# Three more buffers for the scan groups' convolution input, VectorE's chunk 0 additions moved ahead of a convolution, and two PSUM evacuations moved ahead of two silus

## Chip, cores and metric

The kernel runs on one core of a Trainium2 chip. The metric is the device time of one execution in microseconds (us), the median of several runs. The kernel before takes 1314.83 us (3 runs, 1314.35 to 1315.46).

## What is computed

A backbone of two trunk layers over 256 context and 256 latent tokens of width 1024, all in one launch. Layer 0 mixes tokens by a bidirectional Mamba-2 scan, layer 1 by differential attention, and each is followed by a SwiGLU FFN. The change lies in the scan of layer 0. Cut to what matters:

```python
def project(h):                                   # h: rmsnorm and modulation of x
    zxbcdt = h @ w_in                             # 1024 -> z 2048, x 2048, B and C 4 x 128 each, dt
    xbc = silu(dwconv_centred(xbc, conv_w, conv_b))   # 5 taps along the tokens, per channel
def ssd_scan(x, dt, a, b, c, h0):                 # chunks of 128 tokens, 4 groups of 8 heads
    cb = einsum('bclgn,bcsgn->bgcls', cc, bc)
    wmat = cb[:, :, None] * _segsum_exp(a_cum)
    y_diag = einsum('bghcls,bcsghp->bclghp', wmat, xd)          # within a chunk
    states = einsum('bclgn,bclghp->cbghpn', bc, xd * decay_states[..., None])
    y_off = einsum('bclgn,cbghpn->bclghp', cc, h_prev) * decay_out[..., None]   # from the state
# y = y_diag + y_off, forward and backward, + x * d_skip, * silu(z), rmsnorm, @ w_out
```

## The kernel before

The weights arrive as units of 128x2048 f32 (1 MB). ScalarE makes the high f16 half `wh` of each (L408), VectorE the low half `wl` (L854), and TensorE multiplies a unit in eight k-steps of six matmuls (`gemm`, L1501 to L1503), which write two PSUM banks.

The scan runs by groups g = 0 to 3. Groups 0 to 2 are a loop of three iterations, in each of which TensorE computes group g's scan and, interleaved with it, the projection of group g+1: four units, k = 0 to 3. Units 0 to 2 give the six pre-activation tiles of group g+1 (tile 0 is B, 1 is C, 2 to 5 are x), two a unit, and unit 3 gives z. Group 3 (`last_group`, `more=False`) has three z units. The scan's small matmuls hang on the k-steps as hooks, so that TensorE meets them in a fixed order: `exponents(c, q)` (L1684, L1688) for chunk c and quarter q, `within(c, hq)` (L1703), the product within chunk c for half hq of the heads, `from_states(c)` (L1714) and `y_turn(c)` (L1725), a transposition. `within(1, 0)` is in the hook after unit 1's last k-step, `y_turn(1)` after k-step 1 of unit 2, `within(2, 0)` after its k-step 5, `y_turn(2)` and two `exponents` after its k-step 7, `within(2, 1)` after k-step 0 of unit 3, `from_states(3)` and `exponents(3, 2)` after its k-step 1, `within(3, 0)` after k-step 2.

Every engine works through an instruction order written by hand, and the engines meet in semaphores alone.

- ScalarE: `exps` (four 128x128 exponentials, L481), `evac_pre` (copies a tile from PSUM to the buffer `pre`, L452), `silu_xbc` (L472), `z_out` (silu of z from PSUM, L488), and `cvt`, the halves of a unit (L408). The exponentials and the silus have different activation tables, loaded in turn (ACT_TABLE_LOAD).
- VectorE: `conv_tile` (one TENSOR_SCALAR, L1011, and four SCALAR_TENSOR_TENSOR, L1015, from a pre-activation tile into `acc`), `half_chunk(g, c, q)` (L1076, L1078: the factors that `within(c, q)` multiplies), `off` (L1087, L1090), `from_state(g, c)` and `from_chunk(g, c)` (L1060, L1068: add the two parts of y of chunk c into G) and `cvt` (L854).
- GpSimd: the summands of the states, and the gate of a finished group (L1471), which waits for the group's last `from_chunk`. In the last group VectorE's preparation, and with it the first `exponents`, waits for that gate.

Chunk c's product within the chunk goes to the one bank YB, and so `within(c+1, 0)` waits until `from_chunk(g, c)` has read it:

```python
if hq == 0:
    pe.wait_ge(yb_ok, g * NCH + (c + 1))
```

In the loop `pre` has two buffers, tile t using number t mod 2, and the evacuation of tile t waits for the convolution of tile t-2 (`conv_ok`). For group 0's projection, ahead of the loop, `first_pre` gives tiles 2 to 4 three buffers of their own, `px`, in a part of `x` that is not in use until the scan is over. Unit k+1 begins when both tiles of unit k are evacuated (`pre_ok`). A convolution waits for its tile and for the silu of the tile before the last, whose `acc` buffer it takes:

```python
ve.wait_ge(pre_ok, n + 1)
if not (isinstance(g, int) and tile < 2):
    ve.wait_ge(xbc_ok, n - 1)
```

Of the kernel before, what the change touches and what calls it, by code (L numbers as in the profile page):

```python
# [118 lines left out]
def build(nc, cols, keep, stage, xT, wada, wadaT, crow, wdt, wxg, wz, wout, wgu, wdn, wv, wqk, wo, out):  # L119
    ctx = ExitStack()  # L120
    with ctx:
# [209 lines left out]
        HN = {0: 0, 2: 1, 3: 2, 4: 3}  # L331


        def first_pre(tile):

            return px[:, tile - 2] if 2 <= tile < 5 else pre[:, tile % 2]

# [60 lines left out]
        def _(act):  # L398
# [49 lines left out]
            def evac_pre(u, g, tile, b):  # L448

                act.wait_ge(unit_done, u.half + (UD + 2))  # L450
                act.wait_ge(conv_ok, g * 6 + (tile + 1))
                act.activation(pre[:, tile % 2, :, 2:258], GB[b][:, :].rearrange("p (s t) -> p s t", s=2), ACT.Copy,  # L452
                               scale=1.0 / (WS * AS)).then_inc(pre_ok, 1)

            def evac_first(u, tile, b):

                act.wait_ge(unit_done, u.half + (UD + 2))
                if tile == 5:
                    act.wait_ge(conv_ok, 2 + 2)
                act.activation(first_pre(tile)[:, :, 2:258], GB[b][:, :].rearrange("p (s t) -> p s t", s=2), ACT.Copy,  # L460
                               scale=1.0 / (WS * AS)).then_inc(pre_ok, 1)

            def z_first(k, banks):
# [4 lines left out]
            def silu_xbc(g, tile):  # L468
                act.wait_ge(conv_ok, g * 6 + (tile + 3))
                if tile == 0 and not isinstance(g, int):  # L470
                    act.wait_ge(xD_ok, g * QT)
                act.activation(xbc[:, tile, :], acc[tile % 2], ACT.Silu).then_inc(xbc_ok, 1)  # L472

            def exps(g, c, q):

                n = g * 16 + (4 * c + q)
                d, hq = q % 2, q // 2
                act.wait_ge(d_mm, n + 1)
                act.wait_ge(yd, g * 8 + (2 * c + hq + 1))
                for h in range(4):  # L480
                    i = act.activation(E[:, hq, d, h, :], DB[q % 2][:, h * P:(h + 1) * P], ACT.Exp, scale=1.0 / DS,  # L481
                                       bias=PRg[:, NEGA, 2 * c + d, 4 * hq + h:4 * hq + h + 1])
                i.then_inc(e_ok, 1)
# [34 lines left out]
            def group(g, u):  # L518

                prepare(g, u)  # L520
                exps(g, 0, 2)
                ada_load(g * 2 + (ADA_FIRST + 1), g * 2 + 1)
                first_states(g)
                exps(g, 0, 3)
                evac_pre(u, g + 1, 0, 0)
                evac_pre(u, g + 1, 1, 1)
                ada_parts(g)
                cvt(u.plus(2))
                for q in range(3):
                    exps(g, 1, q)  # L530
                evac_pre(u.plus(1), g + 1, 2, 0)
                evac_pre(u.plus(1), g + 1, 3, 1)
                exps(g, 1, 3)
                silu_xbc(g + 1, 0)
                silu_xbc(g + 1, 1)
                cvt(u.plus(3))
                for q in range(4):
                    exps(g, 2, q)
                silu_xbc(g + 1, 2)
                silu_xbc(g + 1, 3)  # L540
                evac_pre(u.plus(2), g + 1, 4, 0)
                evac_pre(u.plus(2), g + 1, 5, 1)
                cvt(u.plus(4))
                for q in range(4):
                    exps(g, 3, q)
                silu_xbc(g + 1, 4)
                act.wait_ge(g_ok, g * 2 + 1)
                z_out(u.plus(3))
                silu_xbc(g + 1, 5)
# [103 lines left out]

            u = Unit(U_SSD0)
            act.wait_ge(pads_ok, 3)
            evac_first(u, 0, 0)
            evac_first(u, 1, 1)
            cvt(u.plus(2))

            act.wait_ge(dtv, 1)  # L660
# [2 lines left out]
            act.activation(de, de, ACT.Exp, scale=-1.0).then_inc(dta, 1)  # L663
            act.activation(da, cc("alog"), ACT.Exp).then_inc(dta, 1)
            silu_xbc(0, 0)
            evac_first(u.plus(1), 2, 2)
            evac_first(u.plus(1), 3, 3)
            cvt(u.plus(3))
            ldt = PR[:, LDT].rearrange("p c h -> p (c h)")
            act.wait_ge(adt_ok, 1)  # L670
            act.activation(ldt, ldt, ACT.Ln).then_inc(ln_ok, 1)
            silu_xbc(0, 1)
            evac_first(u.plus(2), 4, 0)
            evac_first(u.plus(2), 5, 1)
            cvt(u.plus(4))
            act.wait_ge(at_mm, 1)
            for d in range(2):
# [164 lines left out]
        def _(ve):  # L842
# [155 lines left out]
                lo0(k)  # L998
            cvt(Unit(U_SSD0 + 1))

            def conv_tile(g, tile, src=None):

                src = pre[:, tile % 2] if src is None else src
                n = g * 6 + tile
                base = g * 36 + tile * 6
                cw = cc("conv")
                ac = acc[tile % 2].rearrange("p (s t) -> p s t", s=2)
# [3 lines that stand above are left out]
                ve.tensor_scalar(ac, src[:, :, 0:TC], cw[:, bass.ds(base, 1)], cw[:, bass.ds(base + 5, 1)],  # L1011
                                 ALU.mult, ALU.add).then_inc(conv, 1)
                for j in range(1, 5):
                    ve.wait_ge(conv, n * 4 + j)
                    ve.scalar_tensor_tensor(ac, src[:, :, j:j + TC], cw[:, bass.ds(base + j, 1)], ac, ALU.mult,  # L1015
                                            ALU.add).then_inc(conv if j < 4 else conv_ok, 1)
# [4 lines left out]
            db = cc("dtb")  # L1021
            ve.scalar_tensor_tensor(dx.rearrange("p (c h) -> p c h", c=NCH), OB[0][:, 0:256].rearrange("p (c h) -> p c h", c=NCH),
                                    1.0 / (WS * AS), db[:, None, :].to_broadcast([P, NCH, 64]), ALU.mult, ALU.add).then_inc(dtv, 1)
            conv_tile(0, 0, first_pre(0))
            cvt(Unit(U_SSD0 + 2))
            ve.wait_ge(dta, 2)
            step(ve.tensor_scalar(dr, de, 2.0, None, ALU.add))
# [35 lines left out]
            def from_chunk(g, c):  # L1063

                ve.wait_ge(yd, g * 8 + (2 * c + 4))
                ve.wait_ge(a_free, g * A_PER + (A_YT[c] + 2))
                gs = G[:, bass.ds(g * QT, QT), c * P:(c + 1) * P]
                ve.tensor_tensor(gs, gs, YB[:, :].rearrange("p (q l) -> p q l", q=QT), ALU.add).then_inc(yb_ok, 1)  # L1068
# [57 lines left out]
            def group(g, u, more):  # L1126
# [20 lines left out]
                off(g, 0)  # L1147
                cvt(u.plus(2))
                half_chunk(g, 1, 0)
                if more:  # L1150
                    conv_tile(g + 1, 1)
                else:
                    add_z(1)
                from_state(g, 0)
                from_chunk(g, 0)
                off(g, 1)
                half_chunk(g, 1, 1)
                if more:
# [29 lines left out]
                from_chunk(g, 3)  # L1188

            u = Unit(U_SSD0)  # L1190
            conv_tile(0, 1, first_pre(1))
            cvt(u.plus(3))
            conv_tile(0, 2, first_pre(2))
            cvt(u.plus(4))
            ve.wait_ge(A_mm, 1)
            ve.wait_ge(aexp, 2)
# [5 lines left out]
            for d in range(2):  # L1202
                ve.wait_ge(at_hi, d + 1)
                ve.tensor_tensor(atr[0:AROWS, d, :], (YB, AB)[d][0:AROWS, :], AT[0:AROWS, d, :], ALU.subtract).then_inc(at_rest, 1)
            conv_tile(0, 3, first_pre(3))
            for d in range(2):
                ve.wait_ge(at_mid, 2 * d + 2)
                ve.tensor_tensor(AT[64:AROWS, d, :], atr[64:AROWS, d, :], atm[64:AROWS, d, :], ALU.subtract).then_inc(at_ok, 1)
            conv_tile(0, 4, first_pre(4))
            cvt(u.plus(5))  # L1210
            conv_tile(0, 5, first_pre(5))
            ve.wait_ge(aexp, 3)
            ve.wait_ge(at_ok, 2)
            with ve.Fori(0, NG - 1) as g:
# [803 lines left out]
```

## Time and profile before

| | |
|---|---|
| median of 3 runs | 1314.83 us (1314.35 to 1315.46) |
| the profiled execution: its own time, its span | 1321.15 us, 1319.5 us |
| mean granted TensorE clock | 0.949 |
| TensorE matmul busy | 1183.2 us (90%) |
| VectorE busy | 896.2 us (68%) |
| ScalarE busy | 589.4 us (45%) |
| GpSimd busy | 90.0 us (7%) |

Busy times are of one profiled execution. The three iterations of the scan loop stand at about 96.4 to 180.6, 180.6 to 264.7 and 264.7 to 348.9 us of the span, and group 3 from there to about 432 us. In a timeline, the time in brackets is how long the engine was idle ahead of the instruction, and behind it what ended the idle time.

### The profile page before, as it was taken

How to read it: one execution, taken by the hardware profiler on the slowest of the kernel's cores; microseconds unless marked ns; L12 is line 12 of the kernel's file. 1: busy time of each engine (PE TensorE's matmuls, PEld its weight loads, DVE VectorE, ACT ScalarE, POOL GpSimd, SP SyncE). 2: the span in 40 equal slices, each digit the busy share in tenths (PEclk: the TensorE clock that was granted, in tenths of full speed). 3: DMA queues.
4: the chain of work that ended last, by engine and by line, in shares of the span. 5: the costliest groups of instructions: out<-in, count | busy, mean ns of one | idle time of the engine just before them, and what ended most of it. 6: DMA issues, size and time to landing. Idle time of an engine off the chain costs nothing.

```text
span 1319.5 us, 20163 instructions
## 1 busy us (share of the span) xinstructions
PE 1183.2 (90%) x7132; PEld 677.1 (51%) x7132; DVE 896.2 (68%) x1395; ACT 589.4 (45%) x1028; POOL 90.0 (7%) x102
## 2 busy tenths in 40 slices
PE   4999898898986699699999999997999968799997
PEld 2545354454443344244444444446745537688886
DVE  5695766858766886888787887537256756666554
ACT  5564654645646432333343332223335534566642
POOL 0004023050230000000000000000000000000000
PEclk9999899999998799899999999997999968899998
DMA  9332121121222244164554645321231102355552
GB/s 388 132 101 91 64 108 52 64 95 64 93 100 95 97 164 182 37 254 186 195 203 182 241 142 220 125 97 64 83 109 64 64 0 96 128 195 208 196 197 96
DMA packets 24526, 173.93 MB, mean 132 GB/s; under 512 B 2720, under 2 KB 2720, under 8 KB 5536
## 3 DMA queue, kind: packets, MB, share of 16 engines
q1 hardware_dynamic: 18432, 128.24, 26.5%
q0 software_dynamic: 4608, 33.56, 7.1%
q10 hardware_dynamic: 1440, 11.53, 2.4%
q8 instruction: 28, 0.46, 0.1%
q14 instruction: 18, 0.15, 0.0%
HBM read 172.27 MB, written 1.05 MB: 131 GB/s over the span
## 4 chain that ended last, share of the span: by engine, by line
PE 79%; DVE 13%; ACT 4%; issue 3%; DMA 0%; DVEq 0%; ACTq 0%; POOL 0%; SPq 0%; POOLq 0%
PE bank L1501 21%; PE bank L1503 20%; PE bank L1502 20%; PE bank L1674 2%; DVE wl L854 1%; PE bank L1856 1%; PE bank L1703 1%; PE bank L1870 1%; DVE arena L931 1%; DVE arena L1015 1%; DVE arena L926 1%; PE bank L1714 1%; PE bank L1843 1%; DVE ssq L913 1%; PE bank L1684 1%
## 5 line engine op out<-in xcount | busy, mean ns | idle before, releaser
L1501 PE MATMUL bank<-hh,wh 128*128 128x512 f16 (+1 forms) x1136 | 392.3, 345 | 25.6 <-DVE hl L922 8.1
L854 DVE SCALAR_TENSOR_TENSOR wl<-raw,wh 128x1024 f16<-128x1024 f32 x224 | 267.5, 1209 | 209.6 <-ACT wh L408 207.4
L1502 PE MATMUL bank<-hl,wh 128*128 128x512 f16 (+1 forms) x1136 | 391.1, 344 | 0.0
L1503 PE MATMUL bank<-hh,wl 128*128 128x512 f16 (+1 forms) x1136 | 390.8, 344 | 0.0
L408 ACT ACTIVATE wh<-raw 128x1024 f16<-128x1024 f32 x224 | 229.3, 1043 | 297.7 <-PE bank L1503 233.6
L1501 PE MATMUL bank<-arena,wh 128*128 128x512 f16 (+1 forms) x544 | 182.4, 335 | 7.2 <-DVE arena L1275 2.8
L1502 PE MATMUL bank<-arena,wh 128*128 128x512 f16 (+1 forms) x544 | 182.4, 335 | 0.0
L1503 PE MATMUL bank<-arena,wl 128*128 128x512 f16 (+1 forms) x544 | 182.2, 335 | 0.0
L1501 PEld LDWEIGHTS bank<-hh,wh 128*128 128x128 f16 x1136 | 112.4, 99 | 130.8 <-issue 48.4
L1503 PEld LDWEIGHTS bank<-hh,wl 128*128 128x128 f16 x1136 | 112.3, 99 | 93.1 <-issue 5.2
L1502 PEld LDWEIGHTS bank<-hl,wh 128*128 128x128 f16 x1136 | 112.3, 99 | 81.2 <-issue 8.9
L884 DVE SCALAR_TENSOR_TENSOR arena<-arena,araw 128x1024 bf16<-128x1024 f32 x128 | 149.0, 1219 | 0.2
L481 ACT ACTIVATE arena<-bank,arena 128x128 f32<-128x128 f32 x256 | 71.5, 377 | 99.9 <-PE bank L1688 99.7
L1501 PEld LDWEIGHTS bank<-arena,wh 128*128 128x128 f16 x544 | 53.7, 99 | 49.0 <-issue 7.4
L1015 DVE SCALAR_TENSOR_TENSOR arena<-arena,col 128x512 f32<-128x512 f32 x84 | 67.3, 802 | 11.8 <-DVE arena L1011 3.0
L1503 PEld LDWEIGHTS bank<-arena,wl 128*128 128x128 f16 x544 | 53.7, 99 | 39.6 <-issue 1.1
L1502 PEld LDWEIGHTS bank<-arena,wh 128*128 128x128 f16 x544 | 53.7, 99 | 39.1 <-issue 0.8
L723 ACT ACT_TABLE_LOAD x22 | 28.2, 1283 | 46.2 <-PE bank L1503 45.8
L1076 DVE TENSOR_TENSOR arena<-arena 128x512 f32<-128x512 f32 x32 | 23.5, 735 | 32.7 <-ACT arena L481 32.2
L1514 PE MATMUL bank<-kp,ssq 128*128 128x1 f32 x40 | 8.2, 324 | 41.1 <-DVE ssq L913 41.1
L1484 POOL DMA_DIRECT2D arena<-wadaT x30 | 15.8, 528 | 380.4 <-DVE arena L884 380.4
L1843 PE MATMUL bank<-wh,hh 128*128 128x256 f16 x128 | 36.1, 282 | 5.6 <-DVE hl L922 4.6
(229 smaller groups left out, 1338.3 us busy)
## 6 DMA issues: line engine op xcount, KB each, us to landing
raw<-wgu SPq DMA_DIRECT2D x44, 1024.0 KB, 4.8
arena<-wadaT POOLq DMA_DIRECT2D x32, 1024.0 KB, 5.1
raw<-wdn SPq DMA_DIRECT2D x16, 896.0 KB, 4.6
raw<-wxg SPq DMA_DIRECT2D x12, 1024.0 KB, 5.0
arena<-wada SPq DMA_DIRECT2D x8, 1024.0 KB, 19.6
raw<-wz SPq DMA_DIRECT2D x8, 1024.0 KB, 4.8
araw<-wada ACTq DMA_DIRECT2D x8, 1024.0 KB, 4.8
raw<-wout SPq DMA_DIRECT2D x8, 1024.0 KB, 4.9
```

Of the source, the lines that this page charges most:

```text
L408: act.activation(wh[:, u.slot, a:b], raw[:, u.slot, a:b], ACT.Copy, scale=WS).then_inc(hi_done, 1)
L481: i = act.activation(E[:, hq, d, h, :], DB[q % 2][:, h * P:(h + 1) * P], ACT.Exp, scale=1.0 / DS, bias=PRg[:, NEGA, 2 * c + d, 4 * hq + h: ...
L723: act.activation(sg[:, m, t0:T], GB[m][:, t0:T], ACT.Silu, scale=1.0 / (WS * AS)).then_inc(sg_ok, 1)
L854: ve.scalar_tensor_tensor(wl[:, u.slot, a:b], raw[:, u.slot, a:b], WS, wh[:, u.slot, a:b], ALU.mult, ALU.subtract).then_inc(lo_done, 1)
L884: i = ve.scalar_tensor_tensor(adump[:, 2 * m + c, :], abuf[:, b, m, :], 1.0, araw[:, c * D:(c + 1) * D], ALU.mult, ALU.mult, accum_out=asu ...
L1015: ve.scalar_tensor_tensor(ac, src[:, :, j:j + TC], cw[:, bass.ds(base + j, 1)], ac, ALU.mult, ALU.add).then_inc(conv if j < 4 else conv_ok, 1)
L1076: ve.tensor_tensor(E[:, q, 0], E[:, q, 0], E[:, q, 1], ALU.add).then_inc(tsum, 1)
L1501: pe.matmul(o, wh[:, u.slot, wsl], ahi[:, k, t0:t1], start=st, stop=False)
L1502: pe.matmul(o, wh[:, u.slot, wsl], alo[:, k, t0:t1], start=False, stop=False)
L1503: i = pe.matmul(o, wl[:, u.slot, wsl], ahi[:, k, t0:t1], start=False, stop=en)
L1674: pe.matmul(OB[b][:, :], Bt[:, c * P:(c + 1) * P], xdd[:, k % 2, :], start=True, stop=True).then_inc(o_mm[b], 1)
L1843: pe.matmul(o, hh[:, k, tk], wh[:, u.slot, w_], start=(k == 0), stop=False)
```

## The change

`pre_tile` takes the place of `first_pre` in all groups: tiles 2, 3 and 4 go to the three `px` buffers, and 0, 1 and 5 to `pre`. `evac_pre` takes the place of `evac_first`. The evacuation of tile 0 now waits for the last convolution of the group before, the one of tile 5 for the convolution of tile 1, and those of tiles 1 to 4 for none. On ScalarE, in the loop, the evacuations of tiles 4 and 5 stand in front of the silus of tiles 2 and 3. On VectorE, `from_state(g, 0)` and `from_chunk(g, 0)` stand in front of the convolution of tile 1 (in the last group, in front of `add_z(1)`, two additions to a sum of squares, L913).

```diff
-        def first_pre(tile):
+        def pre_tile(tile):
             return px[:, tile - 2] if 2 <= tile < 5 else pre[:, tile % 2]
...
             def evac_pre(u, g, tile, b):
                 act.wait_ge(unit_done, u.half + (UD + 2))
-                act.wait_ge(conv_ok, g * 6 + (tile + 1))
-                act.activation(pre[:, tile % 2, :, 2:258], GB[b][:, :].rearrange("p (s t) -> p s t", s=2), ACT.Copy,
-                               scale=1.0 / (WS * AS)).then_inc(pre_ok, 1)
-            def evac_first(u, tile, b):
-                act.wait_ge(unit_done, u.half + (UD + 2))
+                if tile == 0:
+                    act.wait_ge(conv_ok, g * 6 + 2)
                 if tile == 5:
-                    act.wait_ge(conv_ok, 2 + 2)
-                act.activation(first_pre(tile)[:, :, 2:258], GB[b][:, :].rearrange("p (s t) -> p s t", s=2), ACT.Copy,
+                    act.wait_ge(conv_ok, g * 6 + (2 + 2))
+                act.activation(pre_tile(tile)[:, :, 2:258], GB[b][:, :].rearrange("p (s t) -> p s t", s=2), ACT.Copy,
                                scale=1.0 / (WS * AS)).then_inc(pre_ok, 1)
...
                 for q in range(4):
                     exps(g, 2, q)
+                evac_pre(u.plus(2), g + 1, 4, 0)
+                evac_pre(u.plus(2), g + 1, 5, 1)
                 silu_xbc(g + 1, 2)
                 silu_xbc(g + 1, 3)
-                evac_pre(u.plus(2), g + 1, 4, 0)
-                evac_pre(u.plus(2), g + 1, 5, 1)
                 cvt(u.plus(4))
...
-            def conv_tile(g, tile, src=None):
-                src = pre[:, tile % 2] if src is None else src
+            def conv_tile(g, tile):
+                src = pre_tile(tile)
...
                 half_chunk(g, 1, 0)
+                from_state(g, 0)
+                from_chunk(g, 0)
                 if more:
                     conv_tile(g + 1, 1)
                 else:
                     add_z(1)
-                from_state(g, 0)
-                from_chunk(g, 0)
                 off(g, 1)
```

## Rows read from the trace of the kernel before

**Rows 1.** The page: the chain that ended last, share of the span.

```profile
PE 79%; DVE 13%; ACT 4%; issue 3%; DMA 0%; DVEq 0%; ACTq 0%; POOL 0%; SPq 0%; POOLq 0%
```

**Rows 2.** Waits in the three loop iterations: who for whom, total us, times, longest.

```profile
PE bank L1703 <- DVE arena L1068: 13.3, 3, 4.4
...
PE bank L1501 <- ACT arena L452: 6.9, 3, 2.7
```

**Rows 3.** Timeline of TensorE, second iteration: start, length, instruction, idle ahead.

```profile
223.69 1.12 PE L1703 MATMUL bank<-arena 128*64 128x128 f32 x8 [4.44 <-DVE arena L1068]
...
228.72 0.60 PE L1725 MATMUL bank<-kp,arena 128*128 128x128 f32 x4
...
238.17 0.66 PE L1703 MATMUL bank<-arena 128*64 128x128 f32 x8
...
245.97 0.39 PE L1501 MATMUL bank<-hh,wh 128*128 128x512 f16 x1 [2.69 <-ACT arena L452]
...
247.49 1.12 PE L1703 MATMUL bank<-arena 128*64 128x128 f32 x8
...
254.39 0.66 PE L1703 MATMUL bank<-arena 128*64 128x128 f32 x8
...
264.46 0.39 PE L1501 MATMUL bank<-hh,wh 128*128 128x512 f16 x1 [1.25 <-ACT arena L488]
```

**Rows 4.** Timeline of VectorE, second iteration.

```profile
218.09 0.54 DVE L1011 TENSOR_SCALAR arena<-arena,col 128x512 f32<-128x512 f32 x1
...
222.16 0.68 DVE L1060 TENSOR_TENSOR arena<-bank,arena 128x512 f32 x1
...
223.55 0.68 DVE L1087 TENSOR_TENSOR arena<-bank,arena 128x512 f32<-128x512 f32 x1
226.99 0.69 DVE L1076 TENSOR_TENSOR arena<-arena 128x512 f32<-128x512 f32 x1 [2.76 <-ACT arena L481]
...
244.12 0.68 DVE L1076 TENSOR_TENSOR arena<-arena 128x512 f32<-128x512 f32 x1
```

**Rows 5.** VectorE by groups from convolution 1 on: second, then third iteration.

```profile
L1076 DVE TENSOR_TENSOR arena<-arena 128x512 f32<-128x512 f32 x5 | 3.4, 688 | 4.1 <-ACT arena L481 4.1
...
L1076 DVE TENSOR_TENSOR arena<-arena 128x512 f32<-128x512 f32 x5 | 3.4, 686 | 2.3 <-ACT arena L481 2.3
...
L1011 DVE TENSOR_SCALAR arena<-arena,col 128x512 f32<-128x512 f32 x5 | 2.7, 541 | 1.2 <-ACT arena L472 0.8 <-ACT arena L452 0.4
```

**Rows 6.** Timeline of ScalarE around the evacuations of tiles 4 and 5.

```profile
241.87 1.28 ACT L472 ACT_TABLE_LOAD   x1
243.16 0.63 ACT L472 ACTIVATE arena<-arena 128x512 f32<-128x512 f32 x1
...
244.77 1.07 ACT L452 ACTIVATE arena<-bank 128x512 f32<-128x512 f32 x2
245.73 2.00 ACT L408 ACTIVATE wh<-raw 128x1024 f16<-128x1024 f32 x2
```

**Rows 7.** Windows behind three waits: us, busy time by engine, granted clock.

```profile
223.69:228.70 5.01, 5.01 (x25) 2.65 (x26) 1.92 (x3) 2.86 (x6) 0.00 (x0) 0.70 0.00 0
...
245.97:250.80 4.83, 4.83 (x20) 2.13 (x21) 4.15 (x7) 4.80 (x10) 0.00 (x0) 0.65 0.00 0
...
329.78:333.10 3.32, 3.32 (x21) 1.64 (x22) 2.74 (x5) 3.29 (x4) 0.00 (x0) 1.00 0.00 0
```

**Rows 8.** Timeline of TensorE: first iteration, and the first matmul behind it.

```profile
138.53 1.12 PE L1703 MATMUL bank<-arena 128*64 128x128 f32 x8 [4.44 <-DVE arena L1068]
...
180.37 0.39 PE L1501 MATMUL bank<-hh,wh 128*128 128x512 f16 x1 [1.25 <-ACT arena L488]
```

**Rows 9.** Timelines of the last group: VectorE, then TensorE.

```profile
382.63 1.48 DVE L913 TENSOR_TENSOR ssq<-ssq,sq 128x512 f32<-128x512 f32 x2
...
385.65 0.66 PE L1703 MATMUL bank<-arena 128*64 128x128 f32 x8 [3.06 <-DVE arena L1068]
```

**Rows 10.** Window of the last group behind that wait.

```profile
385.65:388.80 3.15, 3.15 (x19) 1.62 (x20) 1.12 (x2) 1.14 (x4) 0.00 (x0) 0.73 0.04 16
```

More of the change, by code:

```diff
@@ L655, in _ @@
             act.wait_ge(pads_ok, 3)
-            evac_first(u, 0, 0)
-            evac_first(u, 1, 1)
+            evac_pre(u, 0, 0, 0)
+            evac_pre(u, 0, 1, 1)
             cvt(u.plus(2))
@@ L665, in _ @@
             silu_xbc(0, 0)
-            evac_first(u.plus(1), 2, 2)
-            evac_first(u.plus(1), 3, 3)
+            evac_pre(u.plus(1), 0, 2, 2)
+            evac_pre(u.plus(1), 0, 3, 3)
             cvt(u.plus(3))
@@ L672, in _ @@
             silu_xbc(0, 1)
-            evac_first(u.plus(2), 4, 0)
-            evac_first(u.plus(2), 5, 1)
+            evac_pre(u.plus(2), 0, 4, 0)
+            evac_pre(u.plus(2), 0, 5, 1)
             cvt(u.plus(4))
@@ L1023, in _ @@
                                     1.0 / (WS * AS), db[:, None, :].to_broadcast([P, NCH, 64]), ALU.mult, ALU.add).then_inc(dtv, 1)
-            conv_tile(0, 0, first_pre(0))
+            conv_tile(0, 0)
             cvt(Unit(U_SSD0 + 2))
@@ L1190, in _ @@
             u = Unit(U_SSD0)
-            conv_tile(0, 1, first_pre(1))
+            conv_tile(0, 1)
             cvt(u.plus(3))
-            conv_tile(0, 2, first_pre(2))
+            conv_tile(0, 2)
             cvt(u.plus(4))
@@ L1204, in _ @@
                 ve.tensor_tensor(atr[0:AROWS, d, :], (YB, AB)[d][0:AROWS, :], AT[0:AROWS, d, :], ALU.subtract).then_inc(at_rest, 1)
-            conv_tile(0, 3, first_pre(3))
+            conv_tile(0, 3)
             for d in range(2):
@@ L1208, in _ @@
                 ve.tensor_tensor(AT[64:AROWS, d, :], atr[64:AROWS, d, :], atm[64:AROWS, d, :], ALU.subtract).then_inc(at_ok, 1)
-            conv_tile(0, 4, first_pre(4))
+            conv_tile(0, 4)
             cvt(u.plus(5))
-            conv_tile(0, 5, first_pre(5))
+            conv_tile(0, 5)
             ve.wait_ge(aexp, 3)
```

## The prediction

> **What bounds the kernel now.** I read the page's chain first: TensorE carries 79% of it and VectorE 13% [rows 1], so a time counts only where TensorE waits or its clock is down. The list of waits over the three loop iterations comes next. Two waits in it belong to this change: TensorE's L1703 for VectorE's L1068, once an iteration and 4.4 us each, and L1501 for ScalarE's evacuation L452, once an iteration, 6.9 us in all [rows 2]. The timelines place them. The first is `within(1, 0)`: VectorE has finished `half_chunk(1, 0)` when it starts convolution 1 at 218.09, and TensorE stands idle from 219.25 to 223.69 because the two additions that free YB come behind that convolution [rows 3, 4]. The second is the start of unit 3, behind silus 2 and 3 and their table load on ScalarE [rows 3, 6]. Last, the windows show the clock: behind a long wait it is granted at 0.70 and 0.65, that is at the 1.2 GHz level for part of the time, but behind the third iteration's evacuation wait, of 2.1 us, it stayed at 1.00 [rows 2, 7]. So some waits cost more than their idle time: 5.01 x 0.30 = 1.5 us and 4.83 x 0.35 = 1.7 us in the second iteration [rows 7].
>
> **Part 1: the additions in front of convolution 1.** Nothing is added; the pair takes the convolution's place. It is as long as from 222.16 to 223.55, 1.4 us, and the convolution 4.07 us (218.09 to 222.16) [rows 4]. Their input, `y_turn(0)`, is ready before 218.09 in this trace, so `from_chunk(1, 0)` ends 4.07 us earlier and TensorE restarts at 223.69 - 4.07 = 219.62: 0.4 us of wait is left of 4.44. TensorE gains 4.07 us, and the 1.5 us of low clock if a wait of 0.4 us leaves the clock up. No row has so short a wait; the nearest are 1.25 us, behind which a matmul takes 0.39 us as at full clock (at half clock it would be longer), and the third iteration's 2.1 us, both without loss [rows 2, 3, 7]. So I take none.
>
> Late next is `off(1)`. It stands behind both pieces and so stays at 223.55 to 224.23 [rows 4]. `y_turn(1)` reads what it writes: TensorE would come there at about 223.3 (219.62, and 5.03 us less 1.4 of low clock [rows 3]) and waits about 1.0 us until 224.3. It is then 228.72 - 224.3 = 4.4 us ahead of before.
>
> **Part 2: VectorE from there on.** Before, VectorE waited on the way: 2.76 us for the exponentials of `half_chunk(1, 1)` [rows 4], and 0.8 us for silu 0 (the third iteration's row; the second lost as much), in all 4.1 + 0.8 = 4.9 us to the iteration's end [rows 5]. These inputs now come earlier than VectorE does: ScalarE has the exponentials by about 222, VectorE reaches them at 224.2. So VectorE works without a break from 218.09 on, and that sets TensorE's pace. At `within(2, 0)` VectorE is ahead by 2.76 + 0.8 = 3.5 us and some tenths, so TensorE starts it at 238.17 - 3.6 = 234.6, after waiting some 0.8 us. At `half_chunk(2, 1)` (244.12 to 245.5 [rows 4]) it is still 3.6 us ahead, so done at 241.9.
>
> **Part 3: evacuations 4 and 5 in front of silus 2 and 3, and the buffers.** Each side issues the same instructions. ScalarE finished the exponentials of chunk 2 at 241.87, 3.7 us behind TensorE's 238.17 [rows 3, 6], so now at 234.55 + 3.7 = 238.2; TensorE ends unit 2 at about the same time (one `within`, two k-steps and one `exponents` behind 234.55), and the two evacuations (1.07 us [rows 6]) no longer wait for the table load (1.28 us) and two silus (1.6 us from 243.16 to 244.77, the wait for convolution 3 in it). Unit 3 starts at about 239.5, where TensorE arrives just then: the wait of 2.69 us is gone, and the lead is 245.97 - 239.5 = 6.5 us. It can't be kept. `within(2, 1)`, one k-step (1.3 us) later, needs `half_chunk(2, 1)` at 241.9: a wait of 1.0 us, lead 247.49 - 241.95 = 5.5. Queued behind the evacuations on ScalarE are silu 2, for which convolution 4 waits, and `cvt`. Silu 2 is done at 239.4 + 1.28 + 0.63 = 241.3 [rows 6], and VectorE comes to convolution 4 at 241.8: covered, by 0.5 us only. If that cover goes, each us later delays VectorE by as much. `cvt` starts after silu 3, at 241.9 instead of 245.73 [rows 6], and the exponentials of chunk 3 move up by 3.9 us; `exponents(3, 2)` may wait 0.7 us for them, but `within(3, 0)` would wait as long for VectorE anyhow. There VectorE, 3.8 us ahead, ends `half_chunk(3, 0)` at 248.75: lead 254.39 - 248.75 = 5.6. From here TensorE finds all inputs ready. The next group begins at 264.46 - 5.6 = 258.8; VectorE's last addition starts 4.9 to 5.2 us earlier. The next iteration's first half is led by TensorE, so it moves whole.
>
> What the three added buffers do is let evacuation 3 follow 2 at once, where it waited for convolution 1. Without them the pair's new place would have made unit 2 wait. Their cost is nothing: the same instructions at another address; a loss would only show as longer L452, L1011 or L1015. The dropped waits were, but for tile 3's, over when ScalarE came to them, and the new ones (tiles 0 and 5) are on convolutions long done. SP's queue isn't touched; its loads follow VectorE's `cvt`, which comes earlier. ScalarE's `ada_load` moves with its silu 5, GpSimd's gate with the last addition.
>
> **Part 4: the other iterations and the last group.** I take restart to next group as in the second, 258.82 - 219.62 = 39.2 us. First: 138.53 - 4.07 + 39.2 = 173.7 against 180.37 [rows 8], 6.7 us, as it had more low clock before. Third: VectorE idled only 2.3 + 1.2 = 3.5 us there [rows 5], which is what can be won, 3.5 to 3.7; the last group's preparation hangs on VectorE's last addition, over GpSimd's gate, so that end decides. In the last group `add_z(1)` goes behind the pair: 1.4 us (two L913 of 1.48 us in all [rows 9]) off a wait of 3.06. Behind it the clock was 0.73, 3.15 x 0.27 = 0.85 us [rows 10]; with 1.7 us of wait I expect it to stay up.
>
> **Sum:** 6.7 + 5.6 + 3.7 + 1.4 + 0.85 = 18.3 us, of the profiled execution's 1321.15 us (span 1319.5): 1.4%. The median of the runs is 6.3 us lower; I take the gain over unscaled, 1314.8 - 18 = 1296.8, so 1297.
>
> A price worth setting down: without the silu swap, unit 3 would start near 242.3, but `within(3, 0)` still waits for VectorE until 248.75. By idle time the swap is worth some 0.3 us an iteration, not 2.3; what it mainly saves is the low clock behind that wait.
>
> **Rivals.**
>
> The clock. The change turns two long waits into five or six short ones, 0.4 to 1.05 us, some 3 us apart. For a loss: 2.69 us cost 1.7 us. Against it: 1.25 and one 2.1 us wait cost nothing [rows 3, 7]. If the clock falls once an iteration for 5 us, as now, 1.5 to 1.7 us are lost, part of it where TensorE would wait anyway: 18.3 - 3 x 1.6 - 0.85 = 12.6, 1302 us. The Trainium skill speaks for this rival, in TensorE: Matmul & The Clock Gate, "A second HAM failure mode: psum-queue depth-cycling": an engine that idles briefly but often between groups of matmuls had its clock swing between the levels. By that rule the time is this rival's or the next one's; no row here shows it so far.
>
> Slower: the same, taken to its end. If the short waits hold the array at 1.2 GHz from the first (223.3) to the last (248.75), some 21 us of matmul time becomes 42, less the 4 us of waiting it fills: 17 us an iteration, 51 in all, 1297 + 51 = 1348. It turns the sign once low clock eats 6 us an iteration, 12 us of TensorE's work at 1.2 GHz, twice what a 4.44 us wait brings now.
>
> More. VectorE is not the next bound and all waits vanish: 13.3 + 6.9 idle [rows 2], about 9 of clock, 2.3 of the last group: 31 us, 1284. Against: the 41 us of VectorE work behind 218.09 (46.0 less 4.9 [rows 5]) need to be done.
>
> Less. A late input that I count as ready, silu 2 above all (0.5 us of cover), costs 1 to 2 us an iteration: 13 to 15 us of gain, 1300 to 1302.
>
> **How the numbers follow.** Forecast (gain 15 to 21.5 us) 0.66; clock, once an iteration, 0.13; less 0.12; more 0.04; no effect beyond the measurement, which tells 0.2% (2.6 us) from nothing, 0.02; slower 0.03. The range takes in the first three: low 1293 (18.3, the third iteration too at 5.6, and 1.5 for a clock loss that goes elsewhere), high 1303. Faster 0.95, same 0.02, slower 0.03.
>
> **What would show it.** L1703 behind `half_chunk(1, 0)` waits 0.4 us and not 4.4; a new wait of 1 us for L1087 ahead of L1725; none or tenths for L452; waits near 1 us of L1703 for L1076 or L1068; VectorE without a wait for 40 us; granted clock near 1.00 in the loop's second halves; iterations of about 77.5, 78.5 and 80.5 us instead of 84. It is wrong if the clock drops in these stretches, if convolution 4 waits for silu 2, or if the stages behind the scan give the time back.

## The result, and the profile after

The changed kernel takes 1301.03 us (median of 4 runs, 1300.25 to 1302.79) where the kernel before takes 1315.14 us (4 runs, 1314.35 to 1316.03): 14.1 us less. The ratio is 0.9882, with a 95% interval of 0.9867 to 0.9897. The forecast was 1297, with a range of 1293 to 1303: the time lies in the range, and the gain is about four fifths of the 18 us that were forecast. The two profiled executions stand further apart, 19.6 us (spans of 1319.5 and 1299.9 us); that difference is the subject of a part below.

The edits shift the line numbers by three to five (other kernels' a little differently): L1703 is now L1698, L1068 L1063, L1076 and L1078 are L1071 and L1073, L1087 is L1082, L1725 L1720, L1501 L1496, L452 L455, L472 L467, L481 L476. TensorE's timeline in the second iteration of the kernel after, which answers to [rows 3]:

```profile
211.83 0.66 PE L1698 MATMUL bank<-arena 128*64 128x128 f32 x8 [0.41 <-DVE arena L1063]
...
216.58 0.65 PE L1720 MATMUL bank<-kp,arena 128*128 128x128 f32 x4 [0.95 <-DVE arena L1082]
...
226.88 0.66 PE L1698 MATMUL bank<-arena 128*64 128x128 f32 x8 [0.73 <-DVE arena L1063]
...
231.93 0.39 PE L1496 MATMUL bank<-hh,wh 128*128 128x512 f16 x1
...
234.32 0.66 PE L1698 MATMUL bank<-arena 128*64 128x128 f32 x8 [0.93 <-DVE arena L1073]
...
238.67 0.39 PE L1679 MATMUL bank<-negm,idb 128*128 128x512 bf16 x1 [0.57 <-ACT arena L476]
...
241.23 0.66 PE L1698 MATMUL bank<-arena 128*64 128x128 f32 x8 [0.65 <-DVE arena L1073]
...
251.29 0.39 PE L1496 MATMUL bank<-hh,wh 128*128 128x512 f16 x1 [1.25 <-ACT arena L483]
```

Read it against the plan of the prediction: 0.4 us in place of 4.44 at `within(1, 0)`; 0.95 of a new wait for `off(1)` (forecast 1.0); 0.73 at `within(2, 0)` (0.8); unit 3 at 231.93 without a wait for the evacuations; 0.93 at `within(2, 1)` (1.0); 0.57 for the exponentials (0.7); and 0.65 at `within(3, 0)`, where the plan had TensorE wait for VectorE too. From the restart at 211.83 to the next group at 251.29 are 39.46 us (39.2). The iteration, from the first iteration's end at 172.54 on, is 78.75 us.

VectorE in the same stretch, by groups, which answers to [rows 5]; the last column is its idle time and what ended it:

```profile
L1010 DVE SCALAR_TENSOR_TENSOR arena<-x,col,arena 128x512 f32<-128x512 f32 x12 | 9.0, 751 | 1.8 <-DVE arena L1006 0.2 <-DVE arena L1010 0.2
...
L1071 DVE TENSOR_TENSOR arena<-arena 128x512 f32<-128x512 f32 x5 | 3.4, 687 | 0.1
...
L1006 DVE TENSOR_SCALAR arena<-x,col 128x512 f32<-128x512 f32 x3 | 1.6, 541 | 0.0
```

L1071 (L1076 before), which stood behind ScalarE for 4.1 us, has 0.1 us of idle time now, and L1006, which waited 0.8 us for silu 0 before, none. What idle time is left lies between the taps of a convolution. The convolutions that read `x` in place of `pre` take 541 and 751 ns an instruction, as before.

The windows of the three stretches from restart to next group (us, busy time by engine, granted clock), which answer to [rows 7]:

```profile
211.80:251.30 39.50, 34.39 (x210) 17.06 (x210) 36.01 (x51) 26.02 (x56) 0.00 (x0) 1.00 0.19 69
133.00:172.50 39.50, 34.38 (x209) 17.05 (x209) 36.01 (x52) 26.05 (x56) 0.00 (x0) 1.00 0.20 70
290.60:330.00 39.40, 34.37 (x209) 17.05 (x210) 35.91 (x51) 25.97 (x56) 0.00 (x0) 1.00 0.18 68
```

Six waits of 0.4 to 0.95 us in each left the clock at 1.00. In the last group the wait of 3.06 us [rows 9] is one of 1.66, and the clock behind it, 0.73 before [rows 10], is full:

```profile
367.60:371.00 3.40, 3.36 (x26) 2.13 (x27) 2.62 (x5) 1.14 (x4) 0.00 (x0) 1.00 0.39 164
```

### The profile page after: what moved, and what is told of

Same layout as the page of the kernel before. It is cut to its first block, busy times and chain, and to the rows that moved or that the text cites. A ratio compares the mean times of both kernels' runs of the same rounds, so it can differ in the third digit from the quotient of the medians.

```text
span 1299.9 us, 20157 instructions
## 1 busy us (share of the span) xinstructions
PE 1172.0 (90%) x7132; PEld 671.7 (52%) x7132; DVE 895.7 (69%) x1395; ACT 589.2 (45%) x1028; POOL 90.0 (7%) x102
## 4 chain that ended last, share of the span: by engine, by line
PE 77%; DVE 13%; ACT 4%; issue 4%; DVEq 0%; DMA 0%; ACTq 0%; POOL 0%; SPq 0%; POOLq 0%
PE bank L1496 21%; PE bank L1498 20%; PE bank L1497 20%; PE bank L1669 2%; DVE arena L1010 1%; PE bank L1851 1%; DVE wl L849 1%; PE bank L1865 1%; DVE arena L926 1%; DVE arena L921 1%; PE bank L1698 1%; PE bank L1838 1%; ACT wh L408 1%; PE bank L1840 1%; PE bank L1839 1%
## 5 line engine op out<-in xcount | busy, mean ns | idle before, releaser
L1496 PE MATMUL bank<-hh,wh 128*128 128x512 f16 (+1 forms) x1136 | 388.8, 342 | 18.6 <-DVE hl L917 8.1
L1496 PE MATMUL bank<-arena,wh 128*128 128x512 f16 (+1 forms) x544 | 182.4, 335 | 7.2 <-DVE arena L1270 2.8
L1496 PEld LDWEIGHTS bank<-hh,wh 128*128 128x128 f16 x1136 | 111.7, 98 | 122.0 <-issue 38.3
L476 ACT ACTIVATE arena<-bank,arena 128x128 f32<-128x128 f32 x256 | 71.1, 380 | 90.0 <-PE bank L1683 89.8
L1496 PEld LDWEIGHTS bank<-arena,wh 128*128 128x128 f16 x544 | 53.7, 99 | 49.1 <-issue 7.4
L1509 PE MATMUL bank<-kp,ssq 128*128 128x1 f32 x40 | 8.2, 324 | 40.8 <-DVE ssq L908 40.8
L1010 DVE SCALAR_TENSOR_TENSOR arena<-arena,col 128x512 f32<-128x512 f32 x48 | 40.3, 840 | 6.5 <-DVE arena L1006 2.0
L908 DVE TENSOR_TENSOR ssq<-ssq,sq 128x512 f32<-128x512 f32 (+1 forms) x55 | 34.6, 628 | 8.7 <-ACT sq L440 3.2
```

Source lines behind the costliest of these rows:

```text
L908: ve.tensor_tensor(ssq[:, t0:T], ssq[:, t0:T], sq[:, b, t0:T], ALU.add).then_inc(ssd, 1)
L1496: pe.matmul(o, wh[:, u.slot, wsl], ahi[:, k, t0:t1], start=st, stop=False)
```

## The experiments

The kernel before was run anew beside these experiments, on the same chip. Its medians there were 1316.2, 1316.9 and 1317.5 us, so the ratios compare better than the times do. Each diff is against the changed kernel, but for the needless work, which went into both kernels.

### The kernel before once more

No edit.

> The kernel before, unchanged, for a second trace of it. Against the two profiled executions the change took 19.6 us off the span, against the medians 14 to 15.5 us. Theory: the profiled execution of before (1321.15 us) had more low clock than most; a new trace near 1315 us has the same waits of TensorE to 0.1 us (4.4 and 2.1 to 2.7 us an iteration), and shorter stretches behind them, so loop iterations of 82 to 84 us where they were 84.0, 84.1 and 82.2. Rival: the 5 us lie elsewhere (loads, the stages behind the scan), and the iterations are again 84 us. Time equal to before within 0.2%.

1316.35 us, ratio 1.0008 (0.9995 to 1.0022). The trace itself missed the expectation: it was again of a long execution (1321.05 us, span 1319.4), with iterations of 84.1 us. But this code was executed 31 times in all, and the granted clock of each is known. The six lines below are the four longest and the two shortest; the shortest four all have a clock of 0.956, and no execution lies between 1318.6 and 1320.9 us.

```
time us   span us   granted clock
1321.18   1319.5    0.949
1321.09   1319.4    0.949
1321.05   1319.4    0.951
1320.94   1319.3    0.949
1314.39   1312.7    0.956
1314.20   1312.5    0.956
```

One program, 1314.2 to 1321.2 us, and the long ones are those of low clock. The trace under the prediction was one of the long ones. No short execution of this code was traced; the next run has a trace of a short execution of the kernel that differs from it in the buffers alone.

### Five buffers alone

```diff
-                evac_pre(u.plus(2), g + 1, 4, 0)
-                evac_pre(u.plus(2), g + 1, 5, 1)
                 silu_xbc(g + 1, 2)
                 silu_xbc(g + 1, 3)
+                evac_pre(u.plus(2), g + 1, 4, 0)
+                evac_pre(u.plus(2), g + 1, 5, 1)
...
-                from_state(g, 0)
-                from_chunk(g, 0)
                 if more:
                     conv_tile(g + 1, 1)
...
+                from_state(g, 0)
+                from_chunk(g, 0)
```

> Five buffers alone, all orders as before. Theory: evacuation 3 goes 2.3 us earlier while TensorE waits for the additions anyway: no change, within 0.2% of before, and each iteration as long as before's. Rival: an earlier evacuation 3 or a convolution source in x changes something of its own: over 0.2% either way, or L1011/L1015 longer than 0.54 and 0.75 us.

1317.53 us, ratio 1.0003 (0.9991 to 1.0014): nothing, as expected. Its trace has a span of 1314.2 us and the waits of before, but for the evacuation wait of the second iteration, 2.12 us and not 2.69. TensorE in its third iteration:

```profile
302.72 0.66 PE L1698 MATMUL bank<-arena 128*64 128x128 f32 x8 [4.45 <-DVE arena L1063]
...
324.69 0.39 PE L1496 MATMUL bank<-hh,wh 128*128 128x512 f16 x1 [2.13 <-ACT arena L455]
341.56 0.38 PE L1496 MATMUL bank<-hh,wh 128*128 128x512 f16 x1 [1.22 <-issue]
```

And the windows from restart to next group (the column behind the busy times is the granted clock), of this kernel first, then of the kernel before from the run above:

```profile
137.20:177.10 39.90, 36.53 (x209) 18.21 (x209) 32.71 (x46) 25.26 (x54) 0.00 (x0) 0.93 0.16 54
220.50:259.40 38.90, 35.52 (x210) 17.76 (x210) 32.72 (x46) 25.26 (x54) 0.00 (x0) 0.96 0.16 54
302.70:341.50 38.80, 35.49 (x209) 17.76 (x209) 32.64 (x46) 25.26 (x54) 0.00 (x0) 0.96 0.16 54
```

```profile
138.10:180.00 41.90, 38.50 (x209) 18.86 (x209) 33.30 (x48) 25.35 (x55) 0.00 (x0) 0.88 0.16 51
223.30:264.10 40.80, 36.84 (x209) 18.41 (x209) 33.21 (x48) 25.46 (x55) 0.00 (x0) 0.92 0.15 51
307.50:346.30 38.80, 35.49 (x209) 17.74 (x209) 32.61 (x46) 25.26 (x54) 0.00 (x0) 0.96 0.15 54
```

The same work, with waits that differ by 0.6 us at most, takes 38.8 to 38.9 us where the clock is 0.96 and up to 41.9 where it is 0.88. The first two iterations together are 3.9 us longer in the long execution.

### The silu swap undone

```diff
-                evac_pre(u.plus(2), g + 1, 4, 0)
-                evac_pre(u.plus(2), g + 1, 5, 1)
                 silu_xbc(g + 1, 2)
                 silu_xbc(g + 1, 3)
+                evac_pre(u.plus(2), g + 1, 4, 0)
+                evac_pre(u.plus(2), g + 1, 5, 1)
```

> The changed kernel with the silus of tiles 2 and 3 back in front of evacuations 4 and 5. Theory (VectorE's unbroken work sets the pace): TensorE waits 2.8 us for the evacuations again, but the waits of 0.93 and 0.57 us behind it vanish, and within(3, 0) is late by 0.3 us only: 1 us over the loop, plus 1.6 us wherever the clock falls behind the 2.8 us wait, 3 of them at most. 1302 to 1307 us. Rival (a wait removed is its length won): the swap is worth its 2.3 to 2.8 us an iteration and the clock, 8 to 13 us: 1309 to 1314.

1302.56 us, ratio 0.9896 (0.988 to 0.9913), as expected, and not to be told from the changed kernel's 0.9882 by time. The trace tells more. Unit 3 waits 2.7 us for the evacuations in each iteration, and behind it come the windows

```profile
156.00:160.00 4.00, 3.96 (x16) 1.66 (x17) 3.42 (x6) 3.97 (x7) 0.00 (x0) 0.57 0.00 0
236.70:240.70 4.00, 3.94 (x18) 1.80 (x19) 3.42 (x6) 3.97 (x7) 0.00 (x0) 0.66 0.00 0
317.40:321.40 4.00, 3.98 (x22) 2.00 (x23) 3.42 (x6) 3.97 (x7) 0.00 (x0) 1.00 0.00 0
```

Where the clock stayed up, restart to next group is 39.76 us (294.54 to 334.30), 0.3 us more than with the swap; where it fell, 41.4 us. So 2.7 us of wait are worth 0.3 us of time, plus 1.6 us of clock when it falls.

### The additions back behind convolution 1

```diff
-                from_state(g, 0)
-                from_chunk(g, 0)
                 if more:
                     conv_tile(g + 1, 1)
                 else:
                     add_z(1)
+                from_state(g, 0)
+                from_chunk(g, 0)
```

> The changed kernel with the two additions of chunk 0 back behind convolution 1: five buffers and the silu swap alone. Theory: the 4.4 us wait is back with its clock loss, the evacuation wait is gone, but within(2, 1) then waits 0.9 us for VectorE and within(3, 0) again, and 2.0 us an iteration are left; 1.7 us of clock where it fell behind the evacuation wait. Gain over before 6 to 9 us: 1306 to 1309. Rival (waits add up one by one): 6.9 us of idle and 3.4 of clock, 10 us: 1305 or less; or nothing, when VectorE already sets the pace before the change.

1315.17 us, ratio 0.9994 (0.9984 to 1.0003). The expectation of 6 to 9 us was wrong, and the rival's last clause right: from behind its waits for the exponentials and for silu 0 on, VectorE set the pace before the change too. The trace, second iteration:

```profile
220.60 0.78 PE L1698 MATMUL bank<-arena 128*64 128x128 f32 x8 [4.45 <-DVE arena L1063]
242.17 0.66 PE L1698 MATMUL bank<-arena 128*64 128x128 f32 x8 [0.35 <-DVE arena L1073]
247.10 0.39 PE L1679 MATMUL bank<-negm,idb 128*128 128x512 bf16 x1 [1.15 <-ACT arena L476]
249.66 0.66 PE L1698 MATMUL bank<-arena 128*64 128x128 f32 x8 [0.65 <-DVE arena L1073]
```

The wait for the evacuations is gone, and 0.35 + 1.15 + 0.65 = 2.15 us of others stand in its place. Restart to next group is 39.13 us, against 38.90 of the five buffers alone. My 2.0 us an iteration had been read off the long trace, where 1.6 us of it were low clock, and I had added the clock once more.

### Two buffers in the loop

```diff
-            return px[:, tile - 2] if 2 <= tile < 5 else pre[:, tile % 2]
+            return px[:, tile - 2] if first and 2 <= tile < 5 else pre[:, tile % 2]
...
-                if tile == 0:
-                    act.wait_ge(conv_ok, g * 6 + 2)
-                if tile == 5:
-                    act.wait_ge(conv_ok, g * 6 + (2 + 2))
+                if not first:
+                    act.wait_ge(conv_ok, g * 6 + (tile + 1))
+                elif tile == 5:
+                    act.wait_ge(conv_ok, 2 + 2)
```

(`first` is true for group 0's tiles.)

> The changed kernel with the two buffers of before in the loop (evacuation t waits for convolution t-2), the additions and the swap kept. Theory: evacuation 3 now waits for convolution 1 behind the additions, so unit 2 starts about 3 us later, the exponentials of half_chunk(1, 1) come 3 us later and VectorE idles about 1.6 us more, and evacuation 5 waits for convolution 3, which holds unit 3 back by 3 us, long enough for the clock to fall. 3.5 to 5 us an iteration of the gain are lost: 1310 to 1316 us. Rival: the buffers are idle freedom, since VectorE sets the pace: 1301 to 1303 as with five.

1311.97 us, ratio 0.9963 (0.9949 to 0.9976): as expected, 3.8 us an iteration are lost (82.54 us, 176.94 to 259.48). One of the six executions took 1818.53 us at a granted clock of 0.647; it has no trace, and its cause stays open. ScalarE in the second iteration, then TensorE:

```profile
215.94 0.60 ACT L456 ACTIVATE arena<-bank 128x512 f32<-128x512 f32 x1 [0.60 <-PE bank L1499]
220.29 0.60 ACT L456 ACTIVATE arena<-bank 128x512 f32<-128x512 f32 x1 [3.75 <-DVE arena L1011]
220.78 1.13 ACT L477 ACTIVATE arena<-bank,arena 128x128 f32<-128x128 f32 x4
```

```profile
221.02 0.60 PE L1497 MATMUL bank<-hh,wh 128*128 128x512 f16 x1 [3.58 <-ACT arena L456]
```

Evacuation 3 stands 3.75 us behind convolution 1, unit 2 behind it, and so do the exponentials queued behind the evacuation on ScalarE. The second half of the expectation was wrong: evacuation 5 held unit 3 back by 0.3 us, not 3, as everything ahead of it was late already. The clock fell behind the wait of 3.6 us in all three iterations (0.53, 0.66 and 0.72 over the next 5 us), which is part of the 3.8 us.

### `off(1)` in front of convolution 1 as well

```diff
                 from_chunk(g, 0)
+                off(g, 1)
                 if more:
                     conv_tile(g + 1, 1)
                 else:
                     add_z(1)
-                off(g, 1)
```

> The changed kernel with off(1) in front of convolution 1 too. Theory (VectorE's work sets the pace): the 0.95 us wait of y_turn(1) goes, the wait of within(2, 0) for from_chunk(1) grows from 0.73 to about 1.7 us, and an iteration is as long as with the change, 78.7 us to 0.2. Time as the changed kernel, 1301 within 2 us. Rival: TensorE sets it and each removed wait is won: 0.95 us an iteration, 77.8 us.

1304.24 us, ratio 0.9913 (0.9896 to 0.9929). The wait of 0.95 us is gone and the next one is 2.12 us, longer than the 1.7 expected: two short waits became one long one. TensorE in the second iteration:

```profile
228.38 0.66 PE L1698 MATMUL bank<-arena 128*64 128x128 f32 x8 [2.12 <-DVE arena L1063]
241.84 0.39 PE L1679 MATMUL bank<-negm,idb 128*128 128x512 bf16 x1 [1.56 <-ACT arena L476]
```

From restart to next group it is 39.64 us in the third iteration, 0.2 more than with the change, but 41.35 in the second, where the clock fell behind that wait (0.78 in the window from 228.3 to 236.0). The theory held for the idle time. The run's time got no better, rather worse, by more than the 2 us that were expected at most.

### Needless work on VectorE, in both kernels

```diff
                 off(g, 1)
+                if more:
+                    for j in range(2):
+                        ve.wait_ge(xtra, g * 2 + (j + 1))
+                        ve.tensor_tensor(sq[:, 0, :], sq[:, 1, :], sq[:, 1, :], ALU.add).then_inc(xtra, 1)
                 half_chunk(g, 1, 1)
```

> The changed kernel with two needless 128x512 additions on VectorE (0.69 us each, 1.6 to 1.7 us with the wait between them) behind off(1) in each loop iteration. Theory: VectorE has no slack there, TensorE's wait at within(2, 0) grows by 1.6 us and each iteration is 1.5 to 1.7 us longer: 4.5 to 5 us in all, 1305.5 to 1306. Rival: slack somewhere takes it up, 1301 to 1303.

> The same two needless additions in the kernel before. Theory: VectorE waits 2.1 to 2.8 us for the exponentials right behind that place, which hides them: time of before within 0.1%, iterations unchanged, and the wait of L1076 shorter by 1.6 us. Rival: VectorE set the pace before as well, and the kernel is 4.5 to 5 us slower.

In the kernel before: 1316.25 us, ratio 0.9997 (0.9987 to 1.0007), nothing. VectorE there:

```profile
223.94 1.42 DVE L1162 TENSOR_TENSOR sq<-sq 128x512 f32<-128x512 f32 x2
226.56 0.69 DVE L1078 TENSOR_TENSOR arena<-arena 128x512 f32<-128x512 f32 x1 [1.20 <-ACT arena L482]
```

The idle 2.76 us [rows 4] are 1.20 now; the work fell into them. In the changed kernel: 1309.16 us, ratio 0.9951 (0.9935 to 0.9968), 8 to 9 us more than the change alone by the ratios and the times, and more than the 5 expected:

```profile
232.58 0.66 PE L1704 MATMUL bank<-arena 128*64 128x128 f32 x8 [2.08 <-DVE arena L1065]
246.04 0.39 PE L1685 MATMUL bank<-negm,idb 128*128 128x512 bf16 x1 [1.57 <-ACT arena L477]
```

`within(2, 0)` starts 16.40 us behind the restart (216.18) where it was 15.05: 1.35 us of VectorE's work came through. Yet the iteration is 81.79 us (176.88 to 258.67), 3.04 more. The other 1.7 us begin with the clock, which was 0.80 behind the 2.08 us wait (232.5 to 241.0, a loss of 1.7 us), in all three iterations alike. With TensorE late, unit 2, the evacuations and silu 2 are late too, and VectorE stands in front of convolution 4 for it:

```profile
241.38 0.55 DVE L1008 TENSOR_SCALAR arena<-x,col 128x512 f32<-128x512 f32 x1 [1.41 <-ACT arena L468]
```

The same wait of 1.4 us is in the second iteration of the run with `off(1)` moved, where the clock fell, and not in its third. So the prediction's 0.5 us of cover for silu 2 holds only while the clock stays up.

### A new order

TensorE's waits add up to 4.2 us an iteration, and VectorE, without a break behind the restart, idles 5.6 us in the next group's first half. So the order was changed to serve TensorE first and to push a convolution over the border (the diff is shortened to what moves in the loop):

```diff
+                    off(g, 1)
                     conv_tile(g + 1, 1)
-                    off(g, 1)
                     half_chunk(g, 1, 1)
                     conv_tile(g + 1, 2)
                     from_state(g, 1)
-                    cvt(u.plus(3))
                     half_chunk(g, 2, 0)
                     from_chunk(g, 1)
+                    cvt(u.plus(3))
                     off(g, 2)
-                    conv_tile(g + 1, 3)
                     half_chunk(g, 2, 1)
-                    conv_tile(g + 1, 4)
+                    conv_tile(g + 1, 3)
...
                     from_state(g, 3)
-                    conv_tile(g + 1, 5)
+                    conv_tile(g + 1, 4)
                     from_chunk(g, 3)
...
                 prepare(g)
+                conv_tile(g, 5)
                 x_rows(g, 0)
```

On ScalarE `cvt` goes behind `exps(g, 3, 2)`, silu 3 behind `exps(g, 3, 3)`, silu 4 behind `z_out`, and silu 5 behind the copies of B and C in the next group; the last group's wait for the gate of group 2 goes from its start to just ahead of its own first gate.

> A new order for the loop, on top of the change. VectorE: off(1) ahead of convolution 1; from_state(1), half_chunk(2, 0) and from_chunk(1) ahead of cvt; half_chunk(2, 1) ahead of convolution 3; convolution 4 last; convolution 5 behind the next group's preparation. ScalarE: cvt behind the third exponentials of chunk 3, silu 3 behind the fourth, silu 5 in the next group behind the copies of B and C. Theory: VectorE's 41 us behind the restart are as long as before, but its last 4 us now lie in the next group's first half, where VectorE idled 5.6 us; the six waits of 0.4 to 0.95 us shrink to the first one, iterations of 75 to 76.5 us where the changed kernel has 78.75, and 8 to 11 us off the changed kernel: 1290 to 1293. Rival: what is taken from the second half is waited for in the first (x_turn(0) for silu 5, by 4 us), iterations of 78 to 79 us and no gain.

1295.74 us, ratio 0.983 (0.9809 to 0.985): the best of all, faster than the change by 0.5%. Iterations are 76.75 us (168.87 to 245.62), 2.0 less than with the change and 0.25 above what was expected at most. The time missed the expected 1290 to 1293: 5.3 us are gained over the change, not 8 to 11. TensorE's waits in one of them:

```profile
209.75 0.66 PE L1702 MATMUL bank<-arena 128*64 128x128 f32 x8 [0.42 <-DVE arena L1063]
227.35 0.65 PE L1724 MATMUL bank<-kp,arena 128*128 128x128 f32 x4 [0.60 <-DVE arena L1085]
...
253.26 1.09 PE L1649 MATMUL bank<-kp,arena 128*128 128x128 f32 x8 [1.36 <-ACT arena L467]
```

Behind the restart the second half has one wait of 0.6 us left, and the price is the 1.36 us at `x_turn(0)`, for silu 5.

The same without the push over the border (convolution 5 behind 4, silu 5 behind silu 4, the gate's wait where it was):

> The same new order without the deferral: convolution 5 and silu 5 at the end of the iteration. Theory: TensorE's waits in the second half are gone as in the run above, but silu 5 comes at the end of VectorE's 41 us, and the next group's B and C copies behind it on ScalarE: x_turn(0) is held back by 1 to 2 us. Iterations of 76 to 77.5 us: 1293 to 1298. Rival (VectorE's unbroken work sets the iteration's length, whatever its order): 78.5 us or more, and 1301.

1298.37 us, ratio 0.9855 (0.9836 to 0.9874). Inside the loop it is as good, 76.44 us (169.54 to 245.98), with 0.99 us at `exponents(0, 0)`. What it lacks comes at the last group, whose first `exponents` now wait 5.3 us, since VectorE's last addition is late and GpSimd's gate and the preparation hang behind it:

```profile
330.45 0.58 PE L1685 MATMUL bank<-negm,idb 128*128 128x512 bf16 x1 [5.32 <-DVE arena L1092]
```

So the 2 us an iteration come from the order alone, and the push over the border adds nothing inside the loop. Whether it is the push or the later wait for the gate that spares the last group the 5.3 us was not separated. The rival of this run, that VectorE's unbroken work sets the length whatever its order, would have needed 78.5 us and is ruled out: what counts is the work that stands ahead of what TensorE waits for.

## Why the prediction came out as it did

**Part 1** was right, to 0.1 us: restart 4.03 us earlier by the waits (4.44 to 0.41), a new one of 0.95 for `off(1)`. **Part 2**, that VectorE's unbroken work becomes the limit, was right for the order of instructions as it is, and is shown three ways. VectorE has no wait for another engine in the stretch. 1.35 of 1.6 us of needless work go straight into the time there and none of it does before the change. And `off(1)` moved forward wins nothing. The last two runs bound it: with the same work in another order an iteration is 2 us shorter. **Part 3** was right in place and price: the evacuation wait of 2.1 to 2.7 us is worth 0.3 us of idle time and 1.6 us of clock where it falls, and the run without the additions shows that alone it brings nothing measurable. The buffers cost nothing and bring nothing alone, but without them two thirds of the gain are lost (ratio 0.9963 for 0.9882).

What the change brings without the low clock of the long execution can be read from five buffers alone (span 1314.2) and the changed kernel (1299.9), 14.3 us apart. An iteration gains 4.03 us at the restart and gives 0.5 to 0.6 back by the next group (38.84 to 38.90 us before, 39.46 after, except the first: 39.91 and 39.47). That is 3.5 us, which is what VectorE idled there before (2.3 + 1.2 us [rows 5]). The last group gains 1.40 us of wait, as forecast (341.56 and 330.02 at its start are 11.54 us apart, its `within(1, 0)` at 380.58 and 367.64 12.94), and 1.7 us of clock up to its next unit, where 0.85 were forecast from one window that held half of it. By the end of the scan the two are 16.0 us apart (432.54 and 416.54); the stages behind it, which the change doesn't touch, took 1.7 us less with five buffers alone.

**The step that failed** is in Part 4 and the sum: the gain taken over unscaled. The forecast had 6.7 and 5.6 us for the first two iterations and 3.7 for the third. The third measured 3.5. In the first two, the short execution of five buffers alone, whose median is that of before, is 3.9 us shorter than the long one. So most of the 5 us that the forecast had above the third iteration's gain was low clock, which a kernel of the same median was traced without. I saw that the profiled one lay 6.3 us above the median of the runs, and counted its low clock as gain all the same. Between the two profiled executions the sum was near (18.3, and 19.6 measured, of which 1.4 had come about ahead of the restart of the first iteration, where the change does nothing). Between the medians it is 14.1. By three times 3.5 us, 1.4 and 0.85, the same working would have given 12.8 us, and 1302.

That those 6.3 us were the same as the 5 us of gain is not shown. All three traces with the two buffers and the order of before have the long stretches, also that with the needless work, an execution of 1319.05 us (41.8 and 40.8 us in the first two iterations). What that one has less lies behind the scan, as the windows from the scan's end on show, of the kernel before and of this one:

```profile
436.20:1319.40 883.20, 813.23 (x4842) 488.72 (x4842) 591.14 (x950) 348.34 (x532) 15.85 (x30) 0.95 0.39 143
437.30:1317.30 880.00, 809.59 (x4842) 486.64 (x4842) 591.54 (x950) 348.64 (x532) 15.90 (x30) 0.96 0.40 143
```

The changed kernel's profiled execution took the long 883.3 us there too. How often an execution of before has the low clock in the loop stays open.

That 1301.03 lies within the range is in part luck: the range reached up to 1303 for a clock loss and for a late silu 2, and neither came.

**The rivals.** The clock rival did not come: with waits of 0.4 to 0.95 us, 2.5 to 10 us apart, the clock was 1.00 in all three stretches. The rule of the Trainium skill that was set beside it (TensorE: Matmul & The Clock Gate, "A second HAM failure mode: psum-queue depth-cycling") is not borne out by these waits. But the prediction had read the rows one-sidedly: it set the third iteration's 2.1 us wait, without loss, against this rival, and left out the first iteration's of the same trace, as long (2.13 us), behind which the clock fell:

```profile
161.85:165.45 3.60, 3.60 (x15) 1.46 (x15) 3.02 (x5) 3.57 (x6) 0.00 (x0) 0.53 0.00 0
```

Silu 2 was in time, as forecast: convolution 4 starts without a wait in the changed kernel.

## What to carry to other kernels

Before you count a wait as won, run the schedule on from its new end until an engine works without a break: while that engine's order stays, its idle time before the change is all that the change can win, here 3.5 us for the 6 to 7 us of waits removed. A wait's low clock is no fixed price. Compare the profiled execution with the runs, and if it is one of the long ones, work the sum out with its low clock and without it. Two short waits can be better than one long one. And where an engine works without a break, what another engine waits for can go ahead of what nobody needs soon.

## What the runs showed of the hardware

The same wait costs clock in one iteration and not in the next. The granted clock fell behind every wait of 4.4 us in the loop (five traces) and behind all three of 3.6 us with two buffers. Behind 2.7 us it fell in the second iteration of before (0.65) and in two of three without the silu swap (0.57, 0.66, 1.00). Behind 2.1 us it fell in the first iteration of before (0.53) and not in the third, in none of three with five buffers alone, in one of three with `off(1)` moved, and in all three with the needless work in the changed kernel; behind the scan's waits of 1.66 us and less in none. The wait of 3.04 us in the last group was followed by 0.67 in the changed kernel and by 1.00 without the silu swap. A fall in the loop cost 1.6 to 1.7 us behind waits of 2.1 to 2.7 us, and 1.5 to 3.1 behind those of 4.4 (the last is 6.70 us at 0.53, in the first iteration of before). What decides between two equal waits is not shown.

Low clock also comes and goes where nothing was changed: the stages behind the scan took from 880.1 to 883.6 us in the twelve traces.

VectorE was slower beside GpSimd. In the new order convolution 5 runs while GpSimd gates the finished group: the first tap took 0.96 us where it takes 0.54, and the four others 4.21 where they take 3.29 to 3.44. VectorE, and GpSimd:

```profile
241.50 0.54 DVE L1006 TENSOR_SCALAR arena<-x,col 128x512 f32<-128x512 f32 x1
...
247.14 0.96 DVE L1006 TENSOR_SCALAR arena<-arena,col 128x512 f32<-128x512 f32 x1 [0.46 <-DVE arena L1091]
248.25 4.21 DVE L1010 SCALAR_TENSOR_TENSOR arena<-arena,col 128x512 f32<-128x512 f32 x4 [0.15 <-DVE arena L1006]
```

```profile
246.53 2.70 POOL L1470 TENSOR_TENSOR arena<-arena 128x512 f32 x2 [47.83 <-DVE arena L1063]
```

That is 0.4 + 0.8 us, nearly the whole 1.36 us that `x_turn(0)` then waits. The DMA was busy there as well, but it isn't the cause: in the changed kernel convolution 5 ran beside 360 GB/s (248 to 250 us) and took the usual 0.54 and 0.75 us an instruction.
